# Sample values of stick-breaking attention moved one step later and spread behind the prompt heads' sums

## What is computed

```python
z = einsum(q, k) / sqrt(64) + bias[h]
log_keep = where(mask, log_sigmoid(-z), 0)          # mask: key strictly before the query
excl = reverse cumulative sum of log_keep, exclusive
wts = where(mask, exp(log_sigmoid(z) + excl), 0)
out = einsum(wts, v)
```

## Time and profile before

| | |
|---|---|
| median of 3 runs | 1880.63 us (1877.53 to 1881.51) |
| profiled execution, its own time | 1876.92 us |
| its span | 1875.3 us |
| PE busy | 1768.7 us, 94% of the span |
| DVE, ACT, POOL busy | 1013.3, 720.7, 402.6 us |
| attention stage, from the first sample score to the last copy | 1176.5 to 1366.1 us |
| mean transfer rate over the span | 101 GB/s |

### The profile page before, as it was taken

One profiled execution on the slowest core, in us unless ns is written; L12 is line 12 of the kernel. 1 busy time (PEld: TensorE's weight loads), 2 busy tenths in 40 slices (PEclk: granted clock), 3 DMA queues, 4 the chain that ended last, 5 costly groups with the idle time before them and its releaser, 6 DMA issues. The chain is left out here.

```text
span 1875.3 us, 36260 instructions
## 1 busy us (share of the span) xinstructions
PE 1768.7 (94%) x13404; PEld 1640.1 (87%) x13404; DVE 1013.3 (54%) x1848; ACT 720.7 (38%) x1239; POOL 402.6 (21%) x580
## 2 busy tenths in 40 slices
PE   8999899999799999999999999788799999999997
PEld 6999788898598999999998998455488999999997
DVE  4663455551537667666226434556536776678224
ACT  4343333331446334335225213445446333335222
POOL 1554344452001222221000000434200222221000
PEclk9999999998899999999999999899899999999999
DMA  4222111100621222222221226787721222222222
GB/s 171 79 78 79 70 35 34 34 20 1 196 73 68 84 84 78 82 86 97 93 85 64 84 77 245 225 315 248 247 69 56 89 78 83 85 78 76 101 89 86
DMA packets 78367, 188.61 MB, mean 101 GB/s; under 512 B 9442, under 2 KB 25186, under 8 KB 77906
## 3 DMA queue, kind: packets, MB, share of 16 engines
q1 hardware_dynamic: 71618, 168.47, 25.9%
q0 software_dynamic: 6672, 19.10, 3.0%
HBM read 176.00 MB, written 11.55 MB: 100 GB/s over the span
## 5 line engine op out<-in xcount | busy, mean ns | idle before, releaser
L674 PE MATMUL PB<-parts,wparts 128*128 128x288 f32 x8664 | 1169.2, 297 | 20.4 <-DVE wparts L643 9.3
L674 PEld LDWEIGHTS PB<-parts,wparts 128*128 128x128 f32 x8664 | 1163.4, 190 | 24.7 <-DVE wparts L643 19.5
L633 ACT ACTIVATE wparts<-ring 128x1024 fp32r<-128x1024 f32 x198 | 209.9, 1060 | 679.0 <-PE PB L674 678.3
L643 DVE TENSOR_TENSOR wparts<-ring,wparts 128x1024 fp32r<-128x1024 f32 x174 | 213.0, 1224 | 271.5 <-ACT wparts L633 262.0
L1033 POOL COPY cnew<-arena 128x2 f32 (+1 forms) x106 | 115.0, 1085 | 341.6 <-DVE arena L958 338.8
L970 DVE SCALAR_TENSOR_TENSOR arena<-arena,ffw 128x512 f32<-128x512 f32 x176 | 133.2, 757 | 21.3 <-DVE arena L971 12.8
L684 PE MATMUL PB<-parts,wparts 128*128 128x288 f32 x648 | 104.7, 310 | 3.9 <-DVE parts L513 3.3
L955 DVE TENSOR_TENSOR arena<-PB,stats 128x288 f32<-128x288 f32 x88 | 40.2, 457 | 125.3 <-PE PB L674 118.8
L684 PEld LDWEIGHTS PB<-parts,wparts 128*128 128x128 f32 x648 | 91.0, 188 | 12.9 <-DVE parts L513 7.3
L1009 DVE SCALAR_TENSOR_TENSOR arena<-arena,dnw 128x512 f32<-128x512 f32 x54 | 58.1, 1076 | 32.8 <-ACT arena L908 27.6
L932 ACT ACTIVATE arena<-arena,ffw 128x512 f32<-128x512 f32 x88 | 63.8, 725 | 29.4 <-issue 16.8
(11 more groups left out here) (299 smaller groups left out, 2129.4 us busy)
## 6 DMA issues: line engine op xcount, KB each, us to landing
ring<-in_w SPq DMA_DIRECT2D x198, 512.0 KB, 3.2
arena<-in_kpages SPq DMA_DIRECT2D x64, 256.0 KB, 7.0
arena<-in_vpages SPq DMA_DIRECT2D x64, 256.0 KB, 5.2
arena<-in_kpages POOLq DMA_DIRECT2D x64, 128.0 KB, 4.4
arena<-in_vpages POOLq DMA_DIRECT2D x64, 128.0 KB, 5.9
membuf<-in_w SPq DMA_DIRECT2D x8, 512.0 KB, 6.1
arena<-in_state_dn SPq DMA_DIRECT2D x6, 512.0 KB, 5.1
o_dns_s<-arena SPq DMA_DIRECT2D x6, 512.0 KB, 3.9
```

What stands on the lines that cost most here:

```text
L633: nc.scalar.activation(wparts[:, 0, k, :], ring[:, k, :], ACT.Copy).then_inc(hi_ready, 1)
L643: nc.vector.tensor_tensor(wparts[:, 1, k, :], ring[:, k, :], wparts[:, 0, k, :].bitcast(F32), ALU.subtract).then_inc(lo_ready, 1)
L674: last = nc.tensor.matmul(dst(b), wparts[:, part, k, block * P:(block + 1) * P], x[:, row_, b * HALF:(b + 1) * HALF], start=start and part ...
```

## The change

Four things move; none is added or taken away.
- **Sample values.** `pe_set_a` of set p-1 now stands in step p: its first half between the sums of head 0 and head 1, its second half behind those of head 1. After the last step both halves of set 5 stand alone. ACT's copies `act_set_o` move with it, to between `act_set_w(p)` and `act_head_w(p, 1)`.
- **Sample scores.** `pe_set_z(p+1)` goes from ahead of `pe_pair_v(p)` to the end of the step. On ACT `act_set_y(p+1)` goes from between the two `act_head_s` to behind both and behind `act_pair_o(p)`.
- **Sample results.** The transposes `pe_set_r(p-1)` go from ahead of `pe_set_t(p)` to behind the prompt scores `pe_pair_z(p+1)`, and wait for o1 and t2 of that step. On ACT the copies `act_set_m(p-1)` go behind the first `act_head_s`.
- **PSUM places.** The new keys' scores zn take columns 256 to 319 of bank 7 in place of 0 to 63, and the transpose t2 goes to bank 6, columns 128 to 255, behind a wait for ACT's o0.

```diff
--- before.py
+++ after.py
@@ -1779,7 +1779,7 @@
         PAIRS = SB_H // 2
         hd = steps("hd", dict(pe="c00 c01 c02 c10 c11 c12 z0 z1 z2 z3 z4 z5 v", act="w0 w1 a0 l0 a1 l1 o",
                               dve="d00 d01 d02 d10 d11 d12 e0 e1 e2 e3 e4 e5 m0 m1 x0 x1"))
-        st = steps("st", dict(pe="r t0 t1 t2 zn a0 a1", act="xw t0 t2 m y0 y1 yn xe xl o0 o1", dve="d t1 k n s c"))
+        st = steps("st", dict(pe="t0 t1 t2 r zn a0 a1", act="xw o0 o1 t0 t2 m y0 y1 yn xe xl", dve="d t1 k n s c"))
         zoff = [0, 512, 896, 1152]
         zP = [xs_[:, 0:1280], xs_[:, 1280:2560], xs_[:, 2560:3840],
               mkv[:, :, :, :, :].rearrange("p l w c n -> p (l w c n)")[:, 0:1280]]
@@ -1917,7 +1917,7 @@
                 pe.wait_ge(st["act"].sem, st["act"].at("t2", k - 1))
             for g in range(4):
                 pair, f = block_of(k, g)
-                last = nc.tensor.matmul(PB[32 * g:32 * g + 32, 7, 0:NS],
+                last = nc.tensor.matmul(PB[32 * g:32 * g + 32, 7, 2 * P:2 * P + NS],
                                         qblk[:, f, 2 * pair:2 * pair + 2, :].rearrange("p b x -> p (b x)"),
                                         kvT[:, f, SEQ:NT], start=True, stop=True)
             last.then_inc(S.sem, S.mark("zn"))
@@ -1925,7 +1925,8 @@
         def pe_set_r(pe, k):
 
             S = st["pe"]
-            pe.wait_ge(st["act"].sem, st["act"].at("o1", k))
+            pe.wait_ge(st["act"].sem, st["act"].at("o1", k + 1))
+            pe.wait_ge(st["act"].sem, st["act"].at("t2", k + 1))
             for bb in range(2):
                 last = nc.tensor.transpose(PB[:, 6, (2 + bb) * P:(3 + bb) * P], oS[:, bb * P:(bb + 1) * P], ident)
             last.then_inc(S.sem, S.mark("r"))
@@ -1939,7 +1940,8 @@
                     last = nc.tensor.transpose(PB[:, 4 + u, c * P:(c + 1) * P], zS[:, (4 * u + c) * P:(4 * u + c + 1) * P],
                                                ident)
                 last.then_inc(S.sem, S.mark(f"t{u}"))
-            nc.tensor.transpose(PB[0:NS, 7, 0:P], zS[:, PAST:ZW], ident).then_inc(S.sem, S.mark("t2"))
+            pe.wait_ge(st["act"].sem, st["act"].at("o0", k))
+            nc.tensor.transpose(PB[0:NS, 6, P:2 * P], zS[:, PAST:ZW], ident).then_inc(S.sem, S.mark("t2"))
 
         def pe_set_a(pe, k, bb):
 
@@ -1966,28 +1968,35 @@
         def pe_sb(pe):
 
             hd["pe"].skip(pe, -1, "c00", "c01", "c02", "c10", "c11", "c12")
-            st["pe"].skip(pe, -1, "r", "t0", "t1", "t2")
+            st["pe"].skip(pe, -1, "t0", "t1", "t2", "r")
             pe_set_z(pe, 0)
             pe_pair_z(pe, 0)
             hd["pe"].skip(pe, -1, "v")
             st["pe"].skip(pe, -1, "a0", "a1")
             for p in range(PAIRS):
                 pe_head_c(pe, p, 0)
+                if p:
+                    pe_set_a(pe, p - 1, 0)
                 pe_head_c(pe, p, 1)
+                if p:
+                    pe_set_a(pe, p - 1, 1)
+                pe_set_t(pe, p)
+                if p + 1 < PAIRS:
+                    pe_pair_z(pe, p + 1)
+                else:
+                    hd["pe"].skip(pe, p, "z0", "z1", "z2", "z3", "z4", "z5")
                 if p:
                     pe_set_r(pe, p - 1)
                 else:
                     st["pe"].skip(pe, 0, "r")
-                pe_set_t(pe, p)
+                pe_pair_v(pe, p)
                 if p + 1 < PAIRS:
-                    pe_pair_z(pe, p + 1)
                     pe_set_z(pe, p + 1)
                 else:
-                    hd["pe"].skip(pe, p, "z0", "z1", "z2", "z3", "z4", "z5")
                     st["pe"].skip(pe, p, "zn")
-                pe_pair_v(pe, p)
-                pe_set_a(pe, p, 0)
-                pe_set_a(pe, p, 1)
+            pe_set_a(pe, SETS - 1, 0)
+            pe_set_a(pe, SETS - 1, 1)
+            st["pe"].skip(pe, SETS, "t0", "t1", "t2")
             pe_set_r(pe, SETS - 1)
 
         def act_head_w(act, p, e):
@@ -2013,7 +2022,7 @@
             nc.scalar.activation(wT[:, 0:4, :], PB[:, 4, :].rearrange("p (c r) -> p c r", c=4),
                                  ACT.Copy).then_inc(S.sem, S.mark("t0"))
             act.wait_ge(st["pe"].sem, st["pe"].at("t2", k))
-            nc.scalar.activation(wT[0:NS, PAGES, :], PB[0:NS, 7, 0:P], ACT.Copy).then_inc(S.sem, S.mark("t2"))
+            nc.scalar.activation(wT[0:NS, PAGES, :], PB[0:NS, 6, P:2 * P], ACT.Copy).then_inc(S.sem, S.mark("t2"))
 
         def act_set_m(act, k):
 
@@ -2044,7 +2053,7 @@
                 nc.scalar.activation(zS[:, 512 * span:512 * span + 512], PB[:, 4 + span, :], ACT.Identity,
                                      bias=bias).then_inc(S.sem, S.mark(f"y{span}"))
             act.wait_ge(st["pe"].sem, st["pe"].at("zn", k - 1))
-            nc.scalar.activation(zS[:, PAST:ZW], PB[:, 7, 0:NS], ACT.Identity, bias=bias).then_inc(S.sem, S.mark("yn"))
+            nc.scalar.activation(zS[:, PAST:ZW], PB[:, 7, 2 * P:2 * P + NS], ACT.Identity, bias=bias).then_inc(S.sem, S.mark("yn"))
 
         def act_set_s(act, k):
             S = st["act"]
@@ -2066,39 +2075,44 @@
         def act_sb(act):
 
             hd["act"].skip(act, -1, "w0", "w1")
-            st["act"].skip(act, -1, "xw", "t0", "t2", "m")
+            st["act"].skip(act, -1, "xw", "o0", "o1", "t0", "t2", "m")
             act.wait_ge(bias_ready, 1)
             act_set_y(act, 0)
             act_set_s(act, 0)
             act_head_s(act, 0, 0)
             act_head_s(act, 0, 1)
             hd["act"].skip(act, -1, "o")
-            st["act"].skip(act, -1, "o0", "o1")
             for p in range(PAIRS):
                 more = p + 1 < PAIRS
                 if p == 0:
                     act_set_w(act, 0)
+                    st["act"].skip(act, 0, "o0", "o1")
                 act_head_w(act, p, 0)
                 if p:
                     act_set_w(act, p)
+                    act_set_o(act, p - 1, 0)
+                    act_set_o(act, p - 1, 1)
                 act_head_w(act, p, 1)
                 act_set_t(act, p)
+                if more:
+                    act_head_s(act, p + 1, 0)
                 if p:
                     act_set_m(act, p - 1)
                 else:
                     st["act"].skip(act, 0, "m")
                 if more:
-                    act_head_s(act, p + 1, 0)
+                    act_head_s(act, p + 1, 1)
+                    act_pair_o(act, p)
                     act_set_y(act, p + 1)
-                    act_head_s(act, p + 1, 1)
                     act_set_s(act, p + 1)
                 else:
                     hd["act"].skip(act, p, "a0", "l0", "a1", "l1")
                     st["act"].skip(act, p, "y0", "y1", "yn", "xe", "xl")
-                act_pair_o(act, p)
-                act_set_o(act, p, 0)
-                act_set_o(act, p, 1)
-            st["act"].skip(act, SETS, "xw", "t0", "t2")
+                    act_pair_o(act, p)
+            st["act"].skip(act, SETS, "xw")
+            act_set_o(act, SETS - 1, 0)
+            act_set_o(act, SETS - 1, 1)
+            st["act"].skip(act, SETS, "t0", "t2")
             act_set_m(act, SETS - 1)
 
         def dve_head_d(dve, p, e):
```

## The result

| | before | after |
|---|---|---|
| median, 4 runs each | 1881.07 us (1877.53 to 1884.88) | 1863.20 us (1860.15 to 1864.02) |
| profiled execution, its own time | 1876.92 us | 1864.02 us |
| its span | 1875.3 us | 1862.4 us |

The ratio is 0.9902 with a 95% interval of 0.9879 to 0.9924: the changed kernel is faster by 18 us (14 to 23). Timed again on another occasion, it stood at 0.9930 (0.9908 to 0.9951), 13 us (9 to 17). The forecast was 12 us (as a median 1868.7 us, range 1856 to 1880). The two profiled executions differ by 12.9 us, and that is the difference that their traces can explain.

The account below looks back on a forecast made before the run. PE was taken to set the attention stage's pace, interrupted by page waits. Stage -16.8, clock +3.9 and pages +1.0 gave -11.9 us: 1876.92 to 1865.0 profiled, 1868.7 as a median, range 1856 to 1880.

Parts of the forecast that it names:

- What bounds the kernel now: Attention stage: PE sets the pace, interrupted by waits of 15.8 us for V pages and 4.3 for K pages.
- E(0): End of the sums of step 0, E(p) of step p; E(0) to E(5) took 151.5 us, PE needs 119.8.
- Pages: V granules 2 and 3 get about 17 us from release to use instead of 8; page waits fall to 1.0 us.
- DMA share near 0.85: Sign in the profile after: the DMA share is even, near 0.85, with no full and empty steps.
- The chain: From E through ACT's yn and DVE's scan and d00 to PE's c11: PE waits 2.9 us, step 26.9 us.
- The first interval: First step from E(0): no half set and no copy m in the chain, so 24.2 us.
- The tail: Stage end behind E(5): half set, ACT's copies until t2, transposes and values take 13.2 us, where it was 10.3.
- The clock: PE falls to half clock behind the c11 wait in half of five steps, 1.54 us each: 3.9 us, bounds 0 and 7.7.
- PE as the bound: Rival: DVE and ACT keep up, steps take 23.96 us, -31.3 us, 1849.3; chance 0.10.
- Transfers as the bound: Rival: fetches bunch, two full steps keep 33.0 and 35.8 us, 1878.8, no change; chance 0.20.
- The slower clock: Rival: clock falls in every step at the c11 wait, 1872.5 or 1889.8 us; chance 0.15, half of it slower.

Follow-up runs that it names:

- Halves: Kernel before with half of each page fetched and read twice by PE, same matmuls: 0.9921, median 1862.4 us, E(0) to E(5) 137.9 us.
- the fewer transfers: Kernel before with every granule cut to four transfers of 128 KB, fetched part read twice, queues as before: 0.9876, median 1853.4 us.
- Early d0: Changed kernel with DVE's head 0 subtractions of the next pair moved ahead of the samples' s and scan: 0.9915 to before, median 1862.4 us.
- the version with half pages: Changed kernel with half of each page fetched and read twice by PE: 0.9906 to the kernel before, median 1859.1 us.
- the version with both edits: Changed kernel with sample scores back in their old place and DVE's head 0 subtractions ahead of the samples' s and scan: 0.9884 to before, median 1855.7 us.
- the scores in the middle: Changed kernel with sample scores back in their old place on PE and ACT, sample values still spread: 0.9898 to before, median 1856.9 us.

## Why the prediction was right

- **What bounds the kernel now** was right in kind: between E(0) and E(5) hardly anything but pages and the clock behind them came on top of PE's 119.8 us. Halves brought three of the five steps to 23.7 to 24.0 us, PE's own time; the other two still held page waits in every version of the kernel before. I had named bytes and POOL's issue time but not priced them apart; the halves and the fewer transfers did that.
- **Pages.** Forecast 1.0 us, measured 1.2, and 1.6 on the second occasion. One reading was off: V granule 2 is wanted at 1306.82 itself and not 0.95 behind it, so the time before was 7.3 us and not 7 to 9. In the changed kernel it is 16.7 (K granule 0 used up at 1263.3, V granule 2 wanted at 1279.98), close to the 17 that were forecast. The sign "DMA share near 0.85" was too low: two steps are at 0.95 to 1.00.
- **The chain.** Forecast from E: e at 4.55, a0 at 9.1, yn at 16.5, n done at 17.9, scan at 21.6, d00 at 24.0, c11 at 24.7, the step 26.9. Measured: 4.6, 9.1, 16.6, 17.9, 21.7, 24.0, 24.7, and 27.1. The sum of the intervals without a fall of the clock is 132.7 against 131.8 forecast. The wait itself was 2.2 us, with about 0.2 more for x0, against 2.9. Early d0 shows that it is DVE's order and no other wait at that place.
- **The first interval** was forecast at 24.2 and is 24.1. **The tail** was forecast at 13.2 and is 14.7 with its late page, 13.3 in the version with half pages.
- **The clock** was the mis-sized term: 3.9 us for half of five falls. The fall priced at 1.54 cost 1.6 us (28.7 against 27.1), but it came once in one execution, not at all in the second, and not at all in the changed kernel with half pages: fourteen of fifteen waits of 1.4 to 2.3 us left the clock at full speed. The forecast put its bound between waits of 2.11 and 2.85 us, and the trace before already held a row against that:

```profile
1239.17 1.94 PE L1913 MATMUL PB<-arena 128*32 128x512 f32 x8 [1.57 <-DMA arena<-in_kpages]
```

  These eight records took 1.94 us, half clock, behind a wait of 1.57 that came 1.1 us of work after another of 1.27. So the length of the last wait alone does not decide. The Trainium skill, "TensorE: Matmul & The Clock Gate", section on the second failure mode (psum-queue depth-cycling), says that short idle times between groups of matmuls can make the clock swing. One of the fifteen waits agrees; a fall in all five steps, which the prediction drew from it, did not come.
- **The time.** The profiled executions gave -12.9 for a forecast of -11.9, closer than the terms: the chain was 0.9 us longer and the tail with its page 0.5, the clock 2.3 cheaper, and these cancel in part. The timed runs gave -18 (14 to 23) and -13 (9 to 17), and a median of 1863.2 for the forecast 1868.7. The forecast lies in the second interval and 2 us outside the first. What made the first larger is not settled. Parts outside the stage move by some us: in the first pair of profiled executions E(0) lies 2.7 us earlier, with no edit ahead of it, and as much is lost again behind the stage; in the second execution of the changed kernel the stage gave -14.0 and the whole -10.3.
- **The rivals.** PE as the bound did not come: DVE and ACT did not keep up. Transfers as the bound came only when the chain was taken away. The share of 0.95 to 1.00 in two steps shows how near they are. The slower clock did not come.

## What to carry to other kernels

When a consumer holds ring slots, ask how long the time is between the release that starts a fetch and the use of what it brings. Three orders of the same transfers show it: 4.9, 7.3 and 16.7 us between release and use went with 29.9, 15.8 and 1.2 us of waits for V pages. Follow such a move through the in-order lists of the other engines: the spread values took 26 us out of the five steps, and 8 to 9 of them were given back because one engine's scan, made late by the moved scores, stood in front of a subtraction that the matmuls needed. Move one thing at a time: in the five steps the part alone was better than the whole.

## What the runs showed of the hardware

- With the page number read from memory just ahead, SP's queue started a transfer 0.82 us behind the last; with the number at hand, 0.52 (64 KB each, DMA share 0.43, 32 in 22.5 us). POOL took 0.63 on average (16 in 10.0) and 0.69 when eight were left (5.5 us), of which the first alone took 1.8. On POOL's queue half as many transfers with the same bytes took 4.5 us off the time from release to use, and landing stayed at 5.0 and 4.8 us.
- Of twelve PE waits of 2.2 to 2.3 us over three executions (the changed kernel twice, and with half pages) one was followed by a fall to 1.2 GHz. In the version with both edits waits of 3.2 and 1.97 us for pages were each followed by one (PEclk 0.94 in both intervals), and in the kernel before one of 1.57. Where the limit lies, these runs do not show; the length of the wait alone is not it.
- With pages of 256 and 128 KB mixed, a DMA share of 1.00 to 1.03 went with 341 to 362 GB/s (the changed kernel's second interval; the second, third and fifth with the scores in the middle).
